# Projections of the second and third pair of heads moved from the projection stage into the mixers, piece by piece, and kept on chip

## The reference

```python
proj = h @ w_in[l]
q_a, f_a, i_a, g_a, z_b, xbc_b, dt_b, u_c = jnp.split(proj, split_idx, axis=-1)
y_a = hgrn2_mixer(q_a, f_a, i_a, g_a, ...)     # 6 heads of 64: gated linear attention
y_b = mamba2_mixer(z_b, xbc_b, dt_b, ...)      # 6 heads of 64, state 128
y_c = s5_mixer(u_c, ...)                       # diagonal state space, 256 channels
mixed = jnp.concatenate([y_a, y_b, y_c], axis=-1) @ w_out[l]
```

## Time and profile before

| | us |
|---|---|
| median of 3 runs | 3611.72 |
| the profiled execution, its own time | 3613.29 |
| its span, in which all rows lie | 3611.3 |
| TensorE busy in the span | 3246.0 (90%) |
| VectorE, ScalarE, GpSimd busy | 1368.7, 794.8, 830.0 |
| stage C from 253.89 us to its end at 507.92: TensorE busy | 253.6 of 254.0 |
| mixers, 507.92 to 871.84: TensorE busy | 213.2 of 363.9 |

### The profile page before, as it was taken

The page is one execution under the profiler, slowest core; times in us unless marked ns, Lnnn a source line. Parts: engine busy times, 40 slices in busy tenths (PEclk is TensorE's granted clock), DMA queues, the critical chain, the costliest instruction groups (busy, mean ns, idle before and its releaser), DMA issues.

```text
span 3611.3 us, 36829 instructions
## 1 busy us (share of the span) xinstructions
PE 3246.0 (90%) x15749; PEld 2595.7 (72%) x15749; DVE 1368.7 (38%) x2110; ACT 794.8 (22%) x1045; POOL 830.0 (23%) x566
## 2 busy tenths in 40 slices
PE   6999967656989999999787989989999899999996
PEld 5556646555868888888685689966668687787784
DVE  1574614542433333334523425421103334334336
ACT  1111132221021111111225622221100332232230
POOL 0223214442121112112221135510111211111113
PEclk8999985556999999999899999989999999999998
DMA  4122111003021111111101110021120111111111
GB/s 138 37 61 65 45 63 38 30 30 128 1 71 50 53 49 47 47 47 47 71 21 36 36 53 13 19 81 42 41 93 14 47 47 47 47 47 47 47 47 70
DMA packets 154738, 181.54 MB, mean 50 GB/s; under 512 B 6768, under 2 KB 131264, under 8 KB 154320
## 3 DMA queue, kind: packets, MB, share of 16 engines
q1 hardware_dynamic: 148432, 167.56, 14.8%
q10 hardware_dynamic: 6144, 11.64, 0.8%
HBM read 159.10 MB, written 20.09 MB: 50 GB/s over the span
## 4 chain that ended last, share of the span: by engine, by line
PE 78%; DVE 6%; POOL 6%; issue 4%; ACT 3%; DMA 3%; SPq 0%; ACTq 0%; DVEq 0%; POOLq 0%
PE bank L127 76%; POOL f L158 5%; DVE f L158 2%; DVE f L166 2%; ACT f L147 2%; PE bank L142 2%; DVE f L163 1%; DMA f<-w_in 1%; ACT r L150 1%; DMA f<-gr_s 1%; ACT L147 1%; DVE r L158 1%; ACT f L150 0%; DMA f<-x 0%; DVE f L187 0%
## 5 line engine op out<-in xcount | busy, mean ns | idle before, releaser
L127 PE MATMUL bank<-r,r 128*128 128x512 f32 (+1 forms) x8784 | 1975.7, 386 | 66.0 <-DVE r L158 52.1
L127 PEld LDWEIGHTS bank<-r,r 128*128 128x128 f32 x8784 | 1596.7, 191 | 435.3 <-issue 54.5
L158 POOL TENSOR_TENSOR f<-f 128x512 f32<-128x512 f32 (+4 forms) x342 | 435.0, 1281 | 2038.1 <-ACT f L147 669.8
L127 PE MATMUL bank<-f,f 128*128 128x128 f32 (+5 forms) x3380 | 780.0, 387 | 41.3 <-POOL f L158 19.1
L127 PEld LDWEIGHTS bank<-f,f 128*128 128x128 f32 x3380 | 546.5, 196 | 251.4 <-issue 191.3
L127 PE MATMUL bank<-f 128*128 128x64 f32 (+6 forms) x2984 | 453.6, 354 | 123.7 <-POOL f L158 47.1
L158 DVE TENSOR_TENSOR f<-f,bank 128x512 f32<-128x512 f32 (+2 forms) x551 | 338.7, 637 | 468.6 <-PE bank L127 467.0
L127 PEld LDWEIGHTS bank<-f 128*128 128x128 f32 (+2 forms) x2984 | 378.9, 241 | 182.1 <-issue 100.3
L166 DVE SCALAR_TENSOR_TENSOR f<-f,f 128x1024 f32<-128x1024 f32 (+2 forms) x165 | 213.3, 1293 | 475.7 <-ACT f L147 452.9
L158 DVE TENSOR_TENSOR r<-f,r 128x512 fp32r<-128x512 f32 (+2 forms) x130 | 172.1, 1324 | 487.4 <-ACT r L150 487.4
L147 ACT ACTIVATE f<-bank 128x512 f32<-128x512 f32 (+3 forms) x203 | 104.9, 518 | 1043.8 <-PE bank L127 1039.8
(11 more groups left out here) (31 smaller groups left out, 468.1 us busy)
## 6 DMA issues: line engine op xcount, KB each, us to landing
f<-w_in SPq DMA_DIRECT2D x25, 1024.0 KB, 5.4
f<-w_up SPq DMA_DIRECT2D x44, 512.0 KB, 5.2
f<-w_mlp_in SPq DMA_DIRECT2D x16, 1024.0 KB, 5.5
f<-w_mlp_out SPq DMA_DIRECT2D x16, 1024.0 KB, 4.8
f<-w_down SPq DMA_DIRECT2D x11, 1024.0 KB, 5.0
f<-w_out SPq DMA_DIRECT2D x8, 1024.0 KB, 12.7
f<-w_in SPq DMA_DIRECT2D x15, 512.0 KB, 7.3
f<-x SPq DMA_DIRECT2D x2, 2048.0 KB, 13.7
```

The source lines that it names most:

```text
L127: return self.g.matmul(out, lhs, rhs, start=start, stop=stop, skip_group_check=True)
L158: return self.g.tensor_tensor(out, a, b, op)
```

## The change

- Only the first pair's ten pieces are still projected in stage C, staged and sent to DRAM; they are now copied without silu. The order of the ten is now f0, f1, fm, q0, q1, v0, v1, vm, g0, g1.
- The second and third pair's pieces become a third generator in the mixers on TensorE (`pe_more`), one piece in each of the rounds 0 to 19, all in bank 7. ScalarE copies each to its place on chip one step later (`act_more`). The third pair's copies also wait until the first pair is done.
- x transposed (XT) and two ring slots are kept through the first 20 rounds. Stage A's tiles move accordingly: QT, KT, QG into ring slots 0 and 1, BT and CB into a stretch of the row parameters, which is loaded after the mixers ("late params"), before w_out. SSD products get banks 4 to 6.
- The third pair's two weight panels are loaded in SyncE's eleventh round (`sp_more`), behind the wait for the second pair's last piece.
- Silu of q and of g becomes a pass of ScalarE in the mixers (q behind the sigmoid, g at level 7), and the gate's multiplication by the norm weights on GpSimd moves from the head of a pair to behind level 7.
- SyncE no longer loads any pair but the first.

```diff
+        self.slot = [0, 1, 2, 3] * 3 + [2, 3]
+def sp_weights(k, g, n):
+    if n >= 4:
+        g.wait_ge(*k.past("w used", n - 4 if n < 12 else n - 2))
...
-    for i in range(3):
...
+    yield from pe_pair(k, g, 0, PB)
...
+def sp_more(k, g):
+    for _ in range(10):
+        yield
+    sp_weights(k, g, 12)
+    sp_weights(k, g, 13)
+
+def pe_more(k, g):
+    c_done(k, g)
+    for i in (1, 2):
+        yield from pe_pair(k, g, i, [7])
+
+def act_more(k, g):
+    S = k.a
+    yield
+    for i in (1, 2):
+        to = {"q": S.Q[i % 2], "f": S.F, "v": S.V[i % 2], "g": S.GT[i % 2]}
+        for n, part in enumerate(PARTS):
...
+            if i == 2:
+                pair_left(k, g, 0)
+            if name == "f":
+                g.wait_ge(*k.past("g", i - 1))
+            g.wait_ge(*k.past("pair", i, n))
+            g.cp(o, k.bank("pair", i, n)[...]).then_inc(*k.drain("pair acts", "pair", i, n))
...
-    B = [4, 5, 6, 7]
+    B = [4, 5, 6]
...
-    weave(steps(pe_hgrn(k, g), 2), pe_ssd(k, g))
+    weave(steps(pe_hgrn(k, g), 2), pe_ssd(k, g), pe_more(k, g))
```

More of the change, by code:

```diff
@@ L317, in __init__ @@
         self.rows = R.take(sum(n for _, n in ROWS))
+        self.late = sum(n for _, n in ROWS) - 1024
         at = 0
@@ L522, in sp_c @@
     g.dma(S.GLU, A["s5_glu_w"].rearrange("(k p) n -> p k n", p=128)).then_inc(*k.land("s5 in", "s5 in"))
[L523 to L529, removed]
+    for n in range(12):
+        sp_weights(k, g, n)
 def project(k, g, S, name, w, cols, h, thread, among, *use):
@@ new lines, in pe_pair @@
+def pe_pair(k, g, i, among):
+    S = k.c
+    na, nb = 8 + 2 * i, 9 + 2 * i
+    ws = {"q": S.panel(k, na, 128), "f": S.panel(k, na, 128, 1024), "v": S.panel(k, nb, 128), "g": S.panel(k, nb, 128, 1024)}
+    g.wait_ge(*k.past("w in", na))
+    g.wait_ge(*k.past("w in", nb))
+    for n, (name, h) in enumerate(PARTS):
+        w = ws[name]
+        if name in "qf":
+            ins = project(k, g, S, name, w, slice(0, 128), h, "proj", among, "pair", i, n)
+        else:
+            b, freed = k.take("proj", among, "pair", i, n)
@@ L941, in pe_proj @@
-        k.also("w used", nb)
+            if h == "meta":
+                ins = g.sum(b[0:NM, 0:128], [(k.XM[:, j, :], w[:, j, :]) for j in range(8)])
+            else:
+                for c in range(4):
+                    ins = g.sum(b[:, 128 * c:128 * c + 128],
+                                [(k.XT[:, j, 512 * h + 128 * c:512 * h + 128 * c + 128], w[:, j, :]) for j in range(8)])
+        ins.then_inc(*k.up("projected", "pair", i, n))
+        if n == len(PARTS) - 1:
+            k.also("w used", na)
+            k.also("w used", nb)
@@ L988, in act_proj @@
         yield
[L989 to L994, removed]
[L995 to L1006 removed]
+    for n, part in enumerate(PARTS):
+        u = use_pair(n)
+        d = part_of(dr[part[0] + "_s"], *part)
+        o = staged(k, g, u)[0:d.shape[0], 0:d.shape[1]]
+        g.wait_ge(*k.past("pair", 0, n))
+        g.cp(o, k.bank("pair", 0, n)[0:d.shape[0], 0:d.shape[1]]).then_inc(*k.drain("proj acts", "pair", 0, n))
+        g.wait_ge(*k.past("drain", "pair", 0, n))
+        store(u, d, o)
+        yield
 def dve_proj(k, g):
@@ new lines, in act_more @@
+def act_more(k, g):
+    S = k.a
+    yield
+    for i in (1, 2):
+        to = {"q": S.Q[i % 2], "f": S.F, "v": S.V[i % 2], "g": S.GT[i % 2]}
+        for n, part in enumerate(PARTS):
+            name, h = part
+            o = part_of(to[name], *part)
+            if i == 2:
+                pair_left(k, g, 0)
+            if name == "f":
+                g.wait_ge(*k.past("g", i - 1))
+            g.wait_ge(*k.past("pair", i, n))
+            g.cp(o, k.bank("pair", i, n)[0:o.shape[0], 0:o.shape[1]]).then_inc(*k.drain("pair acts", "pair", i, n))
+            if h == "meta" or name in "qg" and h == 1:
+                k.also("v in" if name == "v" else f"{name} raw", i)
```

135 lines of the change are left out of this document (62 added, 73 removed).

## The result

The changed kernel takes **3655.5 us** (median of 4 runs, 3654.7 to 3656.1), the kernel before beside it 3613.0 (4 runs, 3609.8 to 3615.6): a ratio of 1.0118, 95% interval 1.0100 to 1.0135. It is slower, as forecast, by 42.5 us where 29 were forecast.

The account below looks back on a forecast made before the run. It took stage C as bound by TensorE and the mixers as a chain through all engines, TensorE its largest part. Mixers +82 and stage C -53.2 gave +29: 3641 us against 3611.7, range 3572 to 3684.

Parts of the forecast that it names:

- Stage C: End of stage C: the y product starts at 407.96 after GpSimd's fourth sum, and the mixers' first reload comes 53.2 us sooner.
- The price of a piece: Mixers, TensorE: a full piece takes 10.1 us, gives 3.5 back through the clock, 6.6 net; a meta piece costs 1.9.
- begun at the lower level: Mixers, TensorE: each full piece starts at the lower clock and so takes 10.1 us, against 7.03 at full clock.
- B: Mixers: the pieces lift TensorE's clock for the whole stage, mean near 0.9; about 3567 us; chance 0.13.
- Rival C, hiding: Mixers: other engines work on while pieces run, some 80 us of TensorE's idle time used; 3600 us; chance 0.20.
- forecast A: Mixers: TensorE's order sets the rounds, a piece costs 6.6 us; range 3618 to 3665 us; chance 0.50.
- Rival D, one bank: Mixers: TensorE idles ahead of pieces until ScalarE's late copy empties bank 7, +32 us, 3673 us; chance 0.17.
- The weights: Ahead of the third pair's f0: four panel loads take 9 us, 3 of them covered, a stall of 6.
- Rival E: Third pair's weight panels take 19 us, +10 and nothing else; no chance of its own, inside the main forecast's range.
- The boundary: First to second pair in the mixers: without SyncE's reloads and GpSimd's gate wait, 27.7 us becomes 17.5, -10.2.
- Smaller edits: Silu of g and three SSD banks +3 us (0 to +12), late row parameters +1 (-1 to +3); q's silu free.
- Behind the mixers: After the mixers: late row parameters go ahead of w_out, less ahead of x at the start, +1 us (-1 to +3).

Follow-up runs that it names:

- the parts-alone run: The kernel before with only the new order of a pair's projections and three banks for SSD products: 3614.6 us, ratio 1.0007.
- the repaired kernel: The changed kernel with ScalarE's copy at the head of its round and the third pair's first weight panel asked for four rounds earlier: 3626.4 us, ratio 1.0044.
- the run with short pieces: The changed kernel with one of eight products in each projection of the second and third pair, the others left out: 3579.2 us, ratio 0.9916.
- the repaired pair: The changed kernel with ScalarE's copy first and the first weight panel early, with whole pieces (3626.4 us) and with one of eight products (3564.2 us).
- copy first: The changed kernel with ScalarE's copy of a piece at the head of its round: 3639.8 us, ratio 1.0084.
- g pieces later: Only the second pair moved into the mixers, pieces at the round's end, w_out loaded first, and its two g pieces three rounds later: 3596.5 us, ratio 0.9964.
- half moved: The changed kernel with only the second pair in the mixers, pieces and copies at round heads; third pair in stage C, four rounds late: 3598.0 us, ratio 0.9963.
- the run with short, repaired pieces: The changed kernel with ScalarE's copy first, the first weight panel early, and one of eight products in each moved projection: 3564.2 us, ratio 0.9869.

## Why the prediction was right, and where its sizes were off

**Stage C: -61.0, forecast -53.2.** The mechanism is the one told: the y product starts when the fourth sum ends, TensorE is idle before it, and 19.9 us of addition and turning back follow (forecast 0.8 + 18.8). Two sizes were off. The sums ended at 401.9 and not 408.0 (6.1 us), because the time was taken from the earlier trace rows as if the change had left it alone, while the new order of the parts moves it: shown by the parts-alone run. And the y products took 8.53 and 9.65 us, not 10.1 each (2.1 us). TensorE's idle time was forecast from 367 and began at 401.94 - 35.85 = 366.1.

**The price of a piece: the term that was too dear.** TensorE's busy time was to grow by 16 x 10.1 + 4 x 1.9 - 16 x 3.5 = 113 us, and grew by 88.6. The views by shape say where the difference lies. The pieces of the changed kernel (records; us in all, mean ns of one):

```profile
L127 PE MATMUL bank<-f,f 128*128 128x512 f32 x128 | 66.6, 680 | 19.7 <-DMA f<-w_in 13.6 <-ACT f L150 6.1
L127 PE MATMUL bank<-f,f 128*128 128x128 f32 x512 | 68.5, 302 | 40.4 <-ACT f L150 40.4
```

A full piece took (66.6 + 68.5) / 16 = 8.4 us and not 10.1. The four meta pieces took 9.2 us. All other work on TensorE, the same 1375 records, took 301.9 - 135.1 - 9.2 = 157.6 us where it took 213.2: 55.6 us came back, 3.5 a piece, just what was forecast. So the step that failed is "begun at the lower level": where a 4-us row of 64-column products is followed by the next piece, the clock stayed at 1.00 from one to the next, and that piece took 7.03 us. It did so in a part of the stage only, mean 0.72, near the 0.65 to 0.7 that was named and far from B's 0.9. That 3.5 came out to the digit is luck in part, since it was worked out for a clock that falls behind each piece; in the repaired kernel the same sum gives 45.3 us, 2.8 a piece.

The rule of the Trainium skill ("TensorE: Matmul & The Clock Gate", section "Why this matters for your kernels") that a TensorE kept continuously busy gets the full clock agrees with the changed kernel's windows at 524 and 532, and not with those of the run with short pieces, busy 4.00 of 4.00 at 0.50 (busy as the profile reads it). For this mix the measurement decides against it, as the row at 588 in the earlier trace rows did.

**Rival C, hiding: fell.** It wanted some 80 us of the idle time used. With both repairs 25.7 us were, near the 113 - 82 = 31 that forecast A counted on; without them the new waits filled it again. Of 78.4 us of added products 8 were covered with whole against short pieces, and 14 in the repaired pair (77.5 against 63.0). The idle time of a chain isn't capacity: it comes where TensorE waits for a product of its own work, passed on through VectorE, ScalarE and GpSimd, and each piece delays that work too.

**Rival D, one bank: true beside A.** It was given as another outcome, and was a term. There are 47.1 us of waits for the copy, of which 12.7 were on the chain (copy first); A took 0, D 32. Idle time that ends with ScalarE's copy was on the prediction's own list of signs that it is wrong, and this sign came.

**The weights: 13.5 us, forecast 6.** The wait was seen, the size was not. The prediction took 7.5 us for the landing of one load and 9 for four; the four took 8.6 us only to be put out, and the piece began 14.9 us after the first of them. Rival E, weights that cost 10 more, was true beside A too, by 7.5.

**The boundary: -0.9 to -5.0 us, forecast -10.2.** "kdt some 18 us behind the last transposes plus the piece" looks right (27.1 us with a piece of 8.5), but the step behind it was wrong. Without a piece it takes 26.8, 26.0 and 22.7 us in three runs (short pieces, g pieces later, half moved), not 17.5. From the scan on it is 13.1 to 13.4 us without a piece and 624.98 - 607.46 = 17.5 in the changed kernel, so g1 costs about 4 there (forecast 5.0), and the boundary itself gained half of what was claimed or less. The prediction took both boundaries for one chain with SyncE's reloads on top of the first. What is late there is a chunk's addition on VectorE, which at the second boundary doesn't stand in front of the differences for kdt. GpSimd's wait for the gate, which the prediction gave to the first boundary alone, stands at the second too (5.24 us, until 744.81). "Late next" was taken from the other boundary and not from what VectorE and GpSimd do at this one.

**Smaller edits: not to be read apart, forecast 4.** The 8.5 us of the run with short, repaired pieces hold them, the boundary, ScalarE's copies, the meta pieces and the eighth product of every piece, with which TensorE was busy for 32.1 us there; three banks are not in it. The silu of q did fit under the scan, as forecast: the exponential behind it begins at 609.82, when the scan from 607.46 has ended. The other parts weren't tried.

**Behind the mixers: +7.5, forecast +1 for the late parameters.** 2.3 us are the wait for w_out behind the parameters' load, 8.18 against 5.93 us, and this wait goes when w_out goes first, though all behind the mixers then took only 0.9 us less. The rest stays open: the same code behind the mixers took 2739.2 us (both repairs), 2741.3, 2743.2, 2744.1 and 2745.9 in the profiled executions of other runs, and 2747.0 in this one, so it may be one execution's.

In sum: 82.3 + 6 - 10.2 + 4 = +82 was forecast for the mixers, and 71.4 + 25.0 = +96.4 measured. Pieces, boundary and small things together (76.1 against the 71.4 of the repaired kernel) were 5 too dear, and the order (6 against 25.0) was 19 too cheap. Within the first, errors cancel: too dear pieces stand beside a boundary that gained too little. The direction and the main cause, pieces that cost most of their length, were right; that the whole lies within 14 us is in part luck.

## What to carry to other kernels

Before moving work into a stage whose engine is half idle, ask what the engine waits for there. If it is a chain that runs through it, added work costs most of what it adds to the engine's busy time (63.0 of 77.5 us and 70.6 of 78.4 here); if it is another engine that runs by itself, as GpSimd's sums at the end of stage C, work of the size of the gap is free (here 60 us of work, which cost 0.4). Cost every operation that the moved work brings (its copy out of the bank, its weights) by what stands in front of it in its engine's order. Putting the copy at the head of its round gained 12.7 us; for the pieces themselves the place in the round made no difference that can be told.

Move the amount that the gain needs. Here the stage shortened by 61 us when 120 us of work left it, and just as much when 60 did, with the other 60 placed in the gaps.

## What the runs showed that was not expected

Pieces of 128x512 and of 128x128 held TensorE's clock at 2.4 GHz through 4 to 6 us of 64-column products between them, seven windows of 4 us in a row from 520 to 548 us, where from 520 to 532 us the same kind of products between short pieces ran at 1.2 GHz with the engine busy throughout. So here dense work sped up what stands around it: the rest of TensorE's work in the mixers, the same 1375 records, took 157.6 us beside whole pieces, 192.3 beside short ones and 213.2 in the kernel before. What exactly the short pieces lacked isn't shown: they too had windows at 1.00.
